# Beta and the l2 norms of q and k put into the decay's exponent and the output norm, in a streaming encoder block

## The reference, cut to what matters

```
q = _l2norm(q) * (DK ** -0.5);  k = _l2norm(k)        # x * rsqrt(sum(x*x) + EPS)
gc = cumsum(g);  decay = exp(where(incl, gc_t - gc_s, -inf))
kb = k * beta
a = where(strict, (kb @ k.T) * decay, 0);  lower = a + eye
u = solve(lower, v * beta);  w = solve(lower, kb * exp(gc))
qk = (q @ k.T) * decay;  q_dec = q * exp(gc);  k_dec = k * exp(gc[-1] - gc)
v_new = u - w @ state;  o = q_dec @ state + qk @ v_new
state = state * exp(gc[-1]) + k_dec.T @ v_new
...
o_gdn = o * rsqrt(mean(o*o) + EPS) * gdn_norm_w * silu(z)
beta = sigmoid(gb);  g = -exp(a_log) * softplus(ga + dt_bias)
```

## Time and profile before

| what | value |
|---|---|
| median of 3 runs | 2776.21 us (2772.47 to 2779.73) |
| profiled execution | 2775.43 us, span 2773.9 us |
| TensorE matmuls | 2680.9 us busy (97%) |
| VectorE | 1467.4 us busy (53%) |
| ScalarE | 1015.7 us busy (37%) |
| GpSimd | 125.7 us busy (5%) |
| mean granted TensorE clock | 0.988 |

### The profile page before, as it was taken

How to read it: one execution, slowest core, us unless ns; L and a number is a source line. 1 busy time by engine, 2 the same in 40 slices (tenths; PEclk the granted TensorE clock), 3 DMA queues, 4 the chain that set the end, 5 groups by cost and what they waited for, 6 DMA issues and landing times.

```text
span 2773.9 us, 38889 instructions
## 1 busy us (share of the span) xinstructions
PE 2680.9 (97%) x13726; PEld 2220.6 (80%) x13726; DVE 1467.4 (53%) x2205; ACT 1015.7 (37%) x1821; POOL 125.7 (5%) x157
## 2 busy tenths in 40 slices
PE   5999999999999999999999999999999999999998
PEld 4778878888878887888887887888888788788887
DVE  6566464364665536435465554634556555563454
ACT  4445332223454533222345453322234544322222
POOL 0011000000001100000000110000000011000000
PEclk9999999999999999999999999999999999999999
DMA  4210123234321012323332001223333200233242
GB/s 184 91 46 1 39 86 99 97 99 145 137 84 39 1 52 86 99 98 111 132 138 76 31 1 61 91 99 99 132 115 132 69 24 1 69 99 99 99 136 76
DMA packets 62027, 233.74 MB, mean 84 GB/s; under 512 B 7232, under 2 KB 7232, under 8 KB 61120
## 3 DMA queue, kind: packets, MB, share of 16 engines
q1 hardware_dynamic: 55728, 203.09, 22.2%
q0 software_dynamic: 6160, 28.84, 2.8%
HBM read 223.52 MB, written 8.39 MB: 84 GB/s over the span
## 4 chain that ended last, share of the span: by engine, by line
PE 79%; issue 17%; ACT 1%; POOL 1%; DVE 1%; POOLq 0%; DVEq 0%; ACTq 0%
PE ps L1092 77%; PE ps L1211 1%; PE ps L1300 1%; POOL pp L320 1%; ACT xi L575 0%; PE ps L1280 0%; POOL xi L330 0%; DVE h_l L1031 0%; DVE acc L676 0%; POOL qkvz L337 0%; DVE eg L998 0%; ACT ti L565 0%; DVE eg L1003 0%; ACT dt L592 0%; DVE h_l L1009 0%
## 5 line engine op out<-in xcount | busy, mean ns | idle before, releaser
L1092 PE MATMUL ps<-h_h,w_h 128*128 128x512 f32 x2016 | 798.4, 396 | 28.1 <-DVE h_l L1031 9.1
L1092 PE MATMUL ps<-h_h,w_l 128*128 128x512 f32 x2016 | 785.6, 390 | 0.0
L1092 PE MATMUL ps<-h_l,w_h 128*128 128x512 f32 x2016 | 785.4, 390 | 0.0
L668 DVE TENSOR_TENSOR w_l<-stage,w_h 128x1024 fp32r<-128x1024 f32 (+1 forms) x385 | 473.9, 1231 | 302.0 <-ACT w_h L367 288.6
L367 ACT CAST w_h<-stage 128x1024 fp32r<-128x1024 f32 (+1 forms) x385 | 399.0, 1037 | 552.8 <-PE ps L1092 543.8
L1092 PEld LDWEIGHTS ps<-h_h,w_h 128*128 128x128 f32 x2016 | 378.7, 188 | 129.1 <-DVE w_l L668 13.6
L1092 PEld LDWEIGHTS ps<-h_l,w_h 128*128 128x128 f32 x2016 | 379.0, 188 | 81.0 <-issue 4.8
L1092 PEld LDWEIGHTS ps<-h_h,w_l 128*128 128x128 f32 x2016 | 378.8, 188 | 79.7
L1092 PE MATMUL ps<-ff_h,w_h 128*128 128x512 f32 x1024 | 400.0, 391 | 0.0
L1092 PE MATMUL ps<-ff_h,w_l 128*128 128x512 f32 x1024 | 398.4, 389 | 0.0
L1092 PE MATMUL ps<-ff_l,w_h 128*128 128x512 f32 x1024 | 398.4, 389 | 0.0
(11 more groups left out here) (155 smaller groups left out, 2430.9 us busy)
## 6 DMA issues: line engine op xcount, KB each, us to landing
stage<-w SPq DMA_DIRECT2D x385, 512.0 KB, 3.3
x_next<-x POOLq DMA_DIRECT2D x20, 512.0 KB, 6.3
xs<-x POOLq DMA_DIRECT2D x4, 2048.0 KB, 8.5
out<-xs POOLq DMA_DIRECT2D x32, 256.0 KB, 2.3
bia<-bias POOLq DMA_DIRECT2D x1, 1536.0 KB, 7.2
cst<-con SPq DMA_DIRECT2D x1, 1152.0 KB, 5.6
prm<-par SPq DMA_DIRECT2D x1, 38.5 KB, 1.8
```

The lines of the kernel that those rows point to most:

```text
L668: dve.tensor_tensor(w_l[:, b, 0:k], stage[:, s, 0:k], w_h[:, b, 0:k].bitcast(F32), ALU.subtract).then_inc(w_lo.sem, 1)
L1092: return pe.matmul(o, a, b, start=start, stop=stop)
```

## The change

The same function is computed in another way:

- q and k are left unnormalised. The squared length of each key is read off the diagonal of the Gram matrix that TensorE forms anyway (`diagonal`: a product with the identity and a sum over the row, both VectorE, on 128x512). Its logarithm (`LSS`) and log beta go into the exponent of `dt`, as a bias per token (`bias_column`), so that beta's rows are no longer put on all partitions: `decay` has four matmuls for a tile where it had eight, and `inverse_input` has one product where it had two.
- The length of q leaves the scores altogether: the output norm gets q's squares, scaled, added to the squares of o (`query_square` on ScalarE, a new `out_square` on VectorE between ScalarE's square and TensorE's mean).
- 5 norm sums are left of 13 (`NORMS`), those of the attention.
- The key's Gram product goes with `decay` (`key_gram`), ahead of `eg`; in pair 0 both move forward between the attention's q units, and the k-times-q product stands before unit U_Z+1.
- The splits of U_PAD and U_OUT move from before level 0 into the levels: in ScalarE's queue behind the attention's exponentials of levels 2 and 3, in VectorE's behind the softmax of levels 2 and 3, ahead of the next level's L965 (L985 after).
- ScalarE's four exponentials of `dt` (`delta`) come behind `bias_column` and, in pair 1, behind the attention's exponentials.

```
-NORMS = 13
+NORMS = 5
@@ ScalarE @@
-                act.activation(eg[:, a], heads(ring(a, 0)), ACT.Exp)...eg_r
+                act.activation(eg[:, a], heads(ring(a, 1)), ACT.Exp)...eg_r
+                wt(B["ssk"], t)
+                act.activation(sm[:, t, LSS], sm[:, t, SS], ACT.Ln, bias=eps[:, 0:1])...lss
+            def delta(t):
+                wt(B["bias_r"], t)
                 for h in range(HEADS):
-                    act.activation(dt_[:, a, h], d1[:, a, h], ACT.Exp, bias=sm[:, t, NGC][:, h:h + 1])
+                    act.activation(dt_[:, a, h], d1[:, a, h], ACT.Exp, bias=sm[:, t, BIAS][:, h:h + 1])
+            def query_square(t):
+                act.activation(q2[:, a], qkvz[:, 0:4, t*P:t*P + P], ACT.Square, scale=Q_SCALE)...q2_r
...
                 attend("before")
+                for a in range(2 if q else 0):
+                    delta(2 * q + a)
...
                 attend("query")
-                if q == 0:
-                    split_hi(g, CONV, U_PAD - CONV, 1)
-                    split_hi(g, CONV, U_OUT - CONV)
                 for l in range(1, LEVELS + 1):
                     ...  # two copies of xi
                     attend(f"level{l - 1}")
+                    if q == 0 and l == 3:
+                        split_hi(g, CONV, U_PAD - CONV, 1)
+                    if q == 0 and l == 4:
+                        split_hi(g, CONV, U_OUT - CONV)
@@ VectorE @@
+            def diagonal(t):
+                wt(B["p_gg"], t)
+                dve.tensor_tensor(xi[:, a], heads(ring(a, 0)), per_head(I), ALU.mult)...dg_r
+                wt(B["dg_r"], t)
+                dve.tensor_reduce(sm[:, t, SS], xi[:, a], AX.X, ALU.add)...ssk
+            def bias_column(t):
+                wt(B["lss"], t)
+                dve.scalar_tensor_tensor(out=sm[:, t, BIAS], in0=sm[:, t, LSS], scalar=-1.0,
+                                         in1=sm[:, t, NB], op0=ALU.mult, op1=ALU.subtract)...bias_r
+                wt(B["d2"], t)
+                dve.tensor_tensor(sm[:, t, DGC], sm[:, t, DGC], sm[:, t, LSS], ALU.subtract)...dgc
             def inverse_input(t):
-                dve.tensor_tensor(d1[:, a], heads(ring(a, 1)), dt_[:, a], ALU.mult)...db_r
-                dve.tensor_tensor(at_[:, a], heads(ring(a, 0)), d1[:, a], ALU.mult)...at_r
+                dve.tensor_tensor(at_[:, a], heads(ring(a, 0)), dt_[:, a], ALU.mult)...at_r
...
                     attend(f"level{l}")
+                    if q == 0 and l == 2:
+                        split_lo(g, CONV, U_PAD - CONV, 1)
+                    if q == 0 and l == 3:
+                        split_lo(g, CONV, U_OUT - CONV)
...
+                def out_square(a):
+                    dve.tensor_tensor(at_[:, a], at_[:, a], q2[:, a], ALU.add)...osq2
                 new_state(0)
+                out_square(0)
                 gated(0)
                 new_state(1)
+                out_square(1)
                 mix_lo(0)
@@ TensorE @@
-                norm_sum(0) ... norm_sum(12)      # one or two behind each small unit
+                norm_sum(j) behind U_AQ + j, norm_sum(4) behind key_gram(1)
             def decay(t):
-                four(heads(ring(a, 0)), lambda o, h: mm(o, cst[0:64, K_SEL + 4 + h, :], tile), B["p_gr"])
-                four(heads(ring(a, 1)), lambda o, h: mm(o, cst[0:64, K_SEL + h, :], tile), B["p_br"])
+                four(heads(ring(a, 1)), lambda o, h: mm(o, cst[0:64, K_SEL + h, :], tile), B["p_gr"])
```

More of the change, by code:

```diff
@@ L495, in _ @@
                     act.copy(aq[:, j], ps[:, A0 + (U_AQ + j) % 2, :]).then_inc(copied.sem, 1)
[L496 to L506, removed]
-                        decay(0)
-                        split_hi(g, CONV, U_Z + 1 - CONV)
-                        decay(1)
-                    norm_root(6 + 2 * j)
+                    norm_root(j)
+                    if j == 2:
+                        decay(0)
+                delta(0)
+                query_square(0)
+                query_square(1)
+                norm_root(PAIRS)
+                act.wait_ge(B1["tok"].sem, B1["tok"].after(g, 1))
+                act.activation(sm[:, :, EGC], sm[:, :, GC], ACT.Exp).then_inc(B1["egt"].sem, 1)
+                decay(1)
+                split_hi(g, CONV, U_Z + 1 - CONV)
+                delta(1)
                 def exps(n):
@@ L929, in _ @@
                             decay(2 * q + a)
+                            diagonal(2 * q + a)
                     attend("before")
+                    for a in range(2 if q else 0):
+                        bias_column(2 * q + a)
                     for a in range(2 if q else 0):
@@ L1243, in w, with rows @@
                         wt(s, 2 * q + a)
[L1245 to L1247 removed]
+                    def rows(i, a):
+                        return part(i, 2 * q + a)
                     attend("before")
@@ L1259, in _ @@
                         unit(g, CONV, U_Z + 1 - CONV, PT, hid)
-                    attend("gram")
-                    for a in range(2):
-                        w(B["db_r"], a)
-                        four(heads(ring(a, 1)), lambda o, h: mm(o, part(1, a)[:, h], part(0, a)[:, h]), B["p_kq"])
                     attend("query")
@@ L1279, in token_rows @@
                         for h in range(HEADS):
-                            last = pe.transpose(rows_bank()[:, h // 2, h % 2], part(i, a)[:, h], I)
+                            last = pe.transpose(rows_bank()[:, h // 2, h % 2], rows(i, a)[:, h], I)
                         last.then_inc(sig.sem, 1)
@@ L1330, in state_and_out @@
                         w(B["vnc"], a)
-                        four(heads(ring(a, 1)), lambda o, h: mm(o, part(1, a)[:, h], d1[:, a, h]), B["p_su"])
+                        four(heads(ring(a, 1)), lambda o, h: mm(o, rows(1, a)[:, h], d1[:, a, h]), B["p_su"])
                         w(B["qd_r"], a)
```

237 lines of the change are left out of this document (123 added, 114 removed).

## The result

The changed kernel takes 2857.73 us (median of 4 runs, 2846.61 to 2865.57) against 2775.36 us before (4 runs, 2772.47 to 2779.73): a ratio of 1.029, 95% interval 1.025 to 1.033. It is 82.4 us slower. Forecast were 2807 us with a range of 2776 to 2832: the direction was right, the time was not, and the range did not hold it. The profiled execution took 2860.09 us, its span is 2858.5 us and its mean granted clock 0.953 where it was 0.988.

A forecast was written before the change was run, and what follows sets the result against it. TensorE, busy 97% of the span, was taken to bound the kernel. Per group -7.7 - 3.3 + 8.0 + 1.3 + 1.3 + 3.6 = +3.2 us gave 2788, plus 19 for clock: 2807 us, range 2776 to 2832.

The forecast's parts named there:

- norm sums to level 0: Small units: sums, decay rows, a wait and reordering, -7.7 us a group; level 0 of pair 0 without its split wait, -3.3.
- levels 3, 4: Pair 0: `d,xi` waits behind the moved casts and splits, +3.1 us at level 3 and +4.9 at level 4, sum +8.0.
- first output norm: VectorE's new sum of squares, also behind `new_state`, delays the mean for a pair's second tile: +1.3 us a group.
- second output norm: At the group's end the same delay passes through root and gate to the first output unit: +1.3 us a group.
- start of pair 1: First `decay` to transposes: more VectorE products and row sums, bias columns and a later `dt`, +3.6 us a group.
- instructions: All terms apart from the clock, summed over a group: +3.2 us, +13 for four groups, giving 2788 us.
- clock in pair 0: Low stretch of level 0 stays and one more comes behind level 4's pause: +4.8 us a group, +19 in all.
- clock elsewhere: Outside pair 0 the forecast charged no extra low clock: 0 us a group.
- second rival: Two extra low-clock stretches a group, the other at pair 1's start after some 4 us of waiting: 2826 us, chance 0.16.
- clock term: One extra low stretch a group in pair 0, 5.9 us less about 1.1 lying in the pause itself: +4.8 us.
- clock stays up: Rival: removing level 0's pause wins 5.9 us a group and no new pause lowers the clock: 2764 us, chance 0.12.
- Splits fit: Rival: ScalarE reaches the casts before its exponentials' inputs arrive, so levels 3 and 4 do not wait: 2756 us, chance 0.05.

The follow-up runs named there:

- e6: Changed kernel with unread fp32 matmuls filling TensorE's pauses ahead of level 0 and at levels 3 and 4 of pair 0: 2773.24 us, ratio 1.000.
- e8: Kernel before with twelve unread fp32 matmuls in TensorE's 2.96 us wait in level 0 of pair 0: 2755.04 us, ratio 0.993.
- e1: Changed kernel with the splits of U_PAD and U_OUT back before level 0 of pair 0: 2775.15 us, ratio 1.001.
- e4: Changed kernel with 11 and 20 unread matmuls in the pauses at levels 3 and 4, the one ahead of level 0 left open: 2806.22 us, ratio 1.010.
- e9: Changed kernel with unread matmuls in the pauses ahead of level 0 and at level 4, only level 3's left open: 2791.98 us, ratio 1.007.
- e10: Changed kernel with unread matmuls in the pauses ahead of level 0 and at level 3, only level 4's left open: 2796.70 us, ratio 1.008.
- e5: e2 with VectorE's second-tile sum of squares ahead of the state, and pair 1's bias columns and `dt` ahead of the attention's step: 2755.28 us, ratio 0.992.
- e2: Changed kernel with VectorE's half of each moved split one level later, ScalarE's half left in its new place: 2771.07 us, ratio 0.998.
- e7: e5 with the k-times-q products behind unit U_Z+1 again, as before the change: 2726.45 us, ratio 0.983.
- e3: Kernel before with only the splits of U_PAD and U_OUT moved to where the change puts them: 2812.75 us, ratio 1.014.

## Why the prediction was wrong

With e6 and e8, which have no low clock in pair 0, the clock of pair 0 can be taken out. By the spans: the changed kernel less e6 is 87.8 us; before less e8 is 20.4; e6 less e8 is 17.2. And 17.2 + 87.8 - 20.4 = 84.6, the difference of the two spans. The 17.2 us are not instructions alone: e6 has 58.0 us of low clock outside pair 0 and e8 16.3. So the rows below take each interval from a group without low clock in it; only the start of pair 1 has no such group, and stands between bounds.

| term, us a group | predicted | measured | from |
|---|---|---|---|
| norm sums to level 0 | -7.7 - 3.3 | -10.9 | eight sums gone; `avr` transposes to `d,xi` 57.6, now 51.1, and five of the sums (0.87 each) lie ahead |
| levels 3, 4 | +8.0 | +7.7 | level 2 to w 24.7, now 32.4 (e6) |
| first output norm | +1.3 | +1.2 | wait 0.69, now 1.92 |
| second output norm | +1.3 | +1.1 | w of pair 1 to last mean 14.3, now 15.5 |
| start of pair 1 | +3.6 | +1.8 to +4.2 | mean to transposes 16.0; 20.2 with a low stretch of 6.8 in it (e1, e4, e9) |
| instructions | +3.2 | +0.9 to +3.3 | sum of the rows above |
| clock in pair 0 | +4.8 | +16.9 | (87.8 - 20.4) / 4 |
| clock elsewhere | 0 | +1.0 to +3.4 | 17.2 / 4 less the instructions |
| sum | +8.0 | +21.2 | 84.6 / 4 |

The lower bound at the start of pair 1 is an estimate: in e9 this interval took 23.4 to 23.8 us with 17.1 us of low clock and 20.2 with 6.8, some 0.33 us for each us, which would leave about 17.9 without any.

*Right.* The reading of the queues held in each place: `d,xi` of level 0 doesn't wait, levels 3 and 4 wait 2.86 and 4.94 (about 3 and 5 were forecast) for a VectorE that itself waits for the cast, a pause of 2.27 stands ahead of `ti,at` (2.7). The instruction terms together come to 0.9 to 3.3 us a group against the 3.2 forecast. The pause at the start of pair 1, which the second rival named (some 4 us), came too, at 3.31.

*The step that failed* is the clock term: "a stretch costs 5.9 us, less about 1.1 [...]: +4.8 in a group", with one stretch kept and one more, each as long as the 13.7 us that before shows. Three things in it were wrong.

First the count. It charged P4 alone, passed over P3 without a reason, though it is about as long as the one pause behind which the fall had been seen, and let P0 pass as the successor of Pd at the old price. e9 shows that P3 brings its own, at 3.6 us a group in level 3 and 4.9 in all; e4 against e6 prices P0 at 8.5 on the average, 7.9 to 12.6 where low clock followed it, and Pd, the longer one, cost 5.1. And no stretch was charged at the start of pair 1, where 6.8 us and then 3.4 came in every group.

Second the length. I used the 13.7 us as if it were a property of a stretch. It lasted 17.1 to 23.9 us behind P0, with TensorE busy throughout, and up to 34.1 us behind P3 and P4. The stage's short matmuls did not end it; that the second pause inside it lengthened it is argued from e9 and e10, where with one of the two it was at most 13.7 and 23.9 us. Two extra stretches, my second rival, would have been 2826; so even two more at the old length fall 32 us short.

Third the bounds. They were "no extra stretch and two". The trace of before had one pause of that kind in a group, and one case carries no spread. It has another of 2.04 us, among the output units (1046.1), which the prediction leaves out and behind which the clock stayed up in all four groups. An honest upper bound was in reach: the whole of pair 0's levels at 1.2 GHz. From `d,xi` of level 0 (871.27) to the end of level 5 are some 43 us, of which 12.6 were low already; 30 us more at the measured 5.9/12.6 are +14 a group, or 2788 + 57 = 2845. With that in sight the range would have reached further, though still not to 2858.

The price of a us, on the other hand, was about right: 5.9/12.6 = 0.47 by a count of records. The spans give 0.42 (87.8 us for 267.8 - 58.0 of low time) and 0.40 (20.4 for 67.4 - 16.3), and e5's runs 0.43. The Trainium skill, TensorE: Matmul & The Clock Gate, § Terms, puts the penalty at the throttled time by one half at this ratio of clocks. The runs here lie below it, at 0.40 to 0.43, which fits that TensorE also waits in these stretches (4.94 us of the 34.1 are P4 itself). The rule that the prediction cites from the Trainium skill, TensorE: Matmul & The Clock Gate, § Why this matters for your kernels, that pauses between bursts bring the low clock back, was borne out more strongly than I gave it weight for: e8 and e6 take away nothing but idle time, and with it went 20.4 and, against e4, 33.9 us.

The rival "clock stays up" (2764) failed on its condition: removing Pd wins 20.4 us, as e8 shows, but P0 stood ahead of it. That the sparse stage as such brings the low clock is excluded by e6 and e8, which have all its short matmuls and no low stretch in pair 0. "Splits fit" is refuted by the waits.

*Open.* Why the same 2.27 us brought low clock in one group of e5, two of e2 and three of e4, and in all four of the changed kernel and e1, was not settled, nor what sets the length of a stretch. The first stretch at the start of pair 1, which every version of the changed kernel still has, stands in or behind a pause of 1.92 to 3.92 us, but no experiment filled these pauses. And not every stretch has a long pause ahead of it: the 3.4 us at the start of pair 1 in the third and fourth groups of before begin at the end of a wait of 0.75 us.

## What to carry to other kernels

When a step is moved into another engine's slack, ask what stands behind it in that queue and what it waits for itself: here a split that waits for a cast went ahead of the one product TensorE needed, and putting it one place later gave all of it back. Price a pause of TensorE at more than its length: of the 84.6 us lost, 31 (four times 7.7) were the waits at levels 3 and 4 themselves, and 67 the clock behind the pauses of pair 0, the savings elsewhere being set against them. Before trusting a clock term, fill the pauses with products that nobody reads and time that: it tells waits from clock in one run, and where needed work can be put into the pause, as in e7, it is the way to a faster kernel.

## What the runs showed of the hardware

- A pause of 2.27 us (P0) was followed by the granted clock at 0.50 in 14 of the 20 groups that have it (4 of 4 in the changed kernel and in e1, 3 in e4, 2 in e2, 1 in e5). The stretch began between 0.4 us before the pause's end and 2.3 us after it, and lasted 13.7 to 27.3 us of short matmuls. The longer pauses of pair 0 were followed by one in all 20 groups looked at: 2.96 us in before, 2.86 in the changed kernel, e3 and e9, 4.98 in e10.
- Shorter pauses brought it at times. In e2 a stretch of 3.4 us began behind the wait of 1.92 us before a mean in all four groups, in e9 one of 17.1 us in three; in the changed kernel none did. A wait of 2.05 us among the output units was followed by 3.4 us of low clock, beginning about 1.2 us after its end, in all four groups of the changed kernel and in none of before:

```profile
1084.28 0.50 PE L1123 MATMUL ps<-h_h,w_h 128*128 128x512 f32 x1 [2.05 <-DVE h_l L1062]
```

- e4 gives TensorE more work than the changed kernel and takes none away, and its span is 54 us shorter.
- A fp32 matmul with 128 columns took 0.23 us of TensorE (20 of them, 40 records, in 4.63 us).
- Run-to-run spread: 30.9 us in e5 (six runs, P0 open), 2.3 in e7, which is e5 with that pause closed, and 1.8 in e8 (five runs each). A closed pair 0 did not always make it small: e6 has 10.5 us in eleven runs.
